# Modulation columns as dot products along the rows on VectorE, without TensorE

## The reference

```
mod = (silu(c) @ ada_w + ada_b).reshape(1, 2, 2, 3, 1024)      # ada_w is 1024 x 12288
for i in range(2):
    shift, scale, gate = mod[:, i, 0, k]
    h = rmsnorm(x, g) * (1 + scale) + shift
    y = short_conv_mixer(h) if i == 0 else ssd_mixer(h)
    x = x + gate * rmsnorm(y, g)
    shift, scale, gate = mod[:, i, 1, k]
    h = rmsnorm(x, g) * (1 + scale) + shift
    x = x + gate * rmsnorm(swiglu_ffn(h), g)
```

## Time and profile before

| | |
|---|---|
| median of three runs | 2212.21 us (2212.01 to 2213.32) |
| span of the profiled execution | 2209.9 us (the page gives no other time of that execution) |
| TensorE busy | 2167.0 us, 98% |
| VectorE, ScalarE, GpSimd busy | 1203.4, 999.4, 973.0 us |
| moved by the DMA engines | 273.88 MB, 124 GB/s on average |
| same in the first tenth | 316, 221, 209, 124 GB/s in slices of 55 us |
| mean granted clock of TensorE | 0.986 |

### The profile page before, as it was taken

How to read it: one execution, slowest core, us unless ns; L and a number is a source line. 1 busy time by engine, 2 the same in 40 slices (tenths; PEclk the granted TensorE clock), 3 DMA queues, 4 the chain that set the end, 5 groups by cost and what they waited for, 6 DMA issues and landing times.

```text
span 2209.9 us, 29015 instructions
## 1 busy us (share of the span) xinstructions
PE 2167.0 (98%) x10456; PEld 1756.4 (79%) x10456; DVE 1203.4 (54%) x1720; ACT 999.4 (45%) x1425; POOL 973.0 (44%) x421
## 2 busy tenths in 40 slices
PE   7999999999999999999999999999999899999998
PEld 5788888888878777778888888888777688888886
DVE  5877665521176877886522221240888755666522
ACT  4324544334445655654543434453555644444332
POOL 3544444446644333334544456666122143444563
PEclk8999999999999999999999999999999999999999
DMA  7653475553315344333232323344221132333232
GB/s 316 221 209 124 147 272 218 178 161 97 115 58 194 115 148 157 115 124 96 77 95 95 96 74 101 109 122 155 87 70 42 36 105 86 104 95 95 79 97 72
DMA packets 74338, 273.88 MB, mean 124 GB/s; under 512 B 8632, under 2 KB 11320, under 8 KB 67849
## 3 DMA queue, kind: packets, MB, share of 16 engines
q1 hardware_dynamic: 70872, 266.77, 36.5%
q10 hardware_dynamic: 3376, 5.90, 0.8%
HBM read 269.24 MB, written 8.12 MB: 126 GB/s over the span
## 4 chain that ended last, share of the span: by engine, by line
PE 76%; issue 14%; POOL 5%; DVE 3%; ACT 1%; DMA 1%; ACTq 0%; SPq 0%; POOLq 0%; DVEq 0%
PE bank L557 61%; POOL wlo L518 5%; PE bank L974 4%; PE bank L1066 2%; PE bank L580 2%; PE bank L1031 1%; PE bank L995 1%; PE bank L622 1%; PE bank L1014 1%; PE bank L584 1%; PE bank L630 1%; PE bank L669 1%; DMA ada_first<-ada_d 1%; DVE x L1624 1%; PE bank L915 1%
## 5 line engine op out<-in xcount | busy, mean ns | idle before, releaser
L518 POOL TENSOR_TENSOR wlo<-raw,whi 128x1024 fp32r<-128x1024 f32 x382 | 927.6, 2435 | 1146.7 <-ACT whi L1104 1146.4
L1104 ACT ACTIVATE whi<-raw 128x1024 fp32r<-128x1024 f32 x382 | 400.5, 1055 | 560.3 <-PE bank L557 537.8
L557 PE MATMUL bank<-h_hi,whi 128*128 128x512 f32 x1608 | 633.0, 394 | 1.9 <-POOL wlo L518 1.9
L557 PE MATMUL bank<-h_hi,wlo 128*128 128x512 f32 x1608 | 626.5, 390 | 0.0
L557 PE MATMUL bank<-h_lo,whi 128*128 128x512 f32 x1608 | 625.8, 389 | 0.0
L557 PEld LDWEIGHTS bank<-h_hi,whi 128*128 128x128 f32 x1608 | 301.9, 188 | 68.3 <-issue 6.3
L557 PEld LDWEIGHTS bank<-h_hi,wlo 128*128 128x128 f32 x1608 | 301.8, 188 | 64.0
L557 PEld LDWEIGHTS bank<-h_lo,whi 128*128 128x128 f32 x1608 | 302.0, 188 | 61.6
L557 PE MATMUL bank<-g_hi,whi 128*128 128x512 f32 x592 | 230.4, 389 | 0.0
L557 PE MATMUL bank<-g_hi,wlo 128*128 128x512 f32 x592 | 230.3, 389 | 0.0
L557 PE MATMUL bank<-g_lo,whi 128*128 128x512 f32 x592 | 230.3, 389 | 0.0
(11 more groups left out here) (357 smaller groups left out, 2985.2 us busy)
## 6 DMA issues: line engine op xcount, KB each, us to landing
raw<-f_in_d SPq DMA_DIRECT2D x88, 512.0 KB, 3.5
raw<-m_d SPq DMA_DIRECT2D x65, 512.0 KB, 3.6
ada_f<-ada_d SPq DMA_DIRECT2D x24, 1024.0 KB, 7.0
raw<-g_in_d SPq DMA_DIRECT2D x44, 512.0 KB, 3.5
raw<-w_in_d SPq DMA_DIRECT2D x41, 512.0 KB, 3.6
csb<-cs_d SPq DMA_DIRECT2D x32, 640.0 KB, 6.3
ada_a<-ada_d SPq DMA_DIRECT2D x16, 1024.0 KB, 4.9
raw<-a_in_d SPq DMA_DIRECT2D x24, 512.0 KB, 6.0
```

Of the source, the lines that this page charges most:

```text
L518: nc.gpsimd.tensor_tensor(wlo[:, s], raw[:, s], whi[:, s].bitcast(F32), ALU.subtract).then_inc(lo_ready, 1)
L557: mm = nc.tensor.matmul(psum[bank][:], w[:, s, kk, :], xs[part == "lo"][:, k, :], start=first and kk == 0 and i == 0, stop=last and kk == ...
L1104: nc.scalar.activation(whi[:, s], raw[:, s], ACT.Copy).then_inc(hi_ready, 1)
```

## The change

- A column of 128 outputs becomes one VectorE instruction: outputs lie in partitions, the 1024 inputs along the row. An STT over 128x1024 multiplies the weights in SBUF by silu(c), which is the same row in all partitions and lies in banks 6 and 7 of PSUM, and the row sum goes to a column of `mod` (`accum_out`). The products are written over the weights and not used.
- Weights come in another order in DRAM: a transfer of 1 MB holds two columns. The amount is the same.
- The bias is added behind a unit on VectorE, in an instruction over 128x4. `modulation`, `first_sum` and `mod_evac` are gone, and nothing of the modulation is on TensorE. Its loop in f_in0 is the one of f_in1.
- c comes by a broadcast transfer to all partitions (128 x 1024), and ScalarE writes silu(c) to PSUM at the start and again ahead of f_in0, since `residual` uses bank 6. The table's matmuls of the third block's bias move from bank 6 to bank 5.
- The first stage goes by k tile: one transfer has the shift and the scale column of tile k, eight transfers in turn with the weight chunks. For each k VectorE does two columns, bias, `ncol` and `scaled(k)`.
- The first root: ScalarE's squares are added by VectorE into `rstd`, TensorE sums them by tokens. ScalarE takes the root straight from PSUM, then splits all four weight chunks, then norms.
- VectorE's loop over f_in0 is written out.

```diff
 # SyncE, start
-            sp.dma_start(vec[:], io["vec"]).then_inc(vec_in, 16)
             for h in range(2):
                 sp.dma_start(x[:, 4 * h:4 * h + 4], ...).then_inc(x_in[h], 16)
+            sp.dma_start(cond[:].rearrange("p a n -> p (a n)"), io["c"].broadcast_to([P, D])).then_inc(c_in, 16)
+            sp.dma_start(vec[:], io["vec"]).then_inc(vec_in, 16)
+            ada_start(0)
             sp.dma_start(kst[:], io["kst"]).then_inc(kst_in, 16)
-            for v in range(2):
+            load(io["a_in"][0], 0)
+            ada_start(1)
+            for v in range(1, 4):
                 load(io["a_in"][v], v)
-            ada_start(0)
-            for v in range(2, 4):
-                load(io["a_in"][v], v)
-            for p in range(1, 4):
-                ada_start(p)
+                ada_start(v + 1)
+            for k in range(5, KD):
+                ada_start(k)
 # SyncE, later units
-                    if h or d == 4:
-                        sp.wait_ge(mod_part, d + it * n)
+                    if d == 4:
+                        sp.wait_ge(col_out, 4)
+                    elif h:
+                        sp.wait_ge(mod_part, d - 4 + it * n)
                     else:
                         sp.wait_ge(ada_half, d - 4 + it * n)
 # TensorE
             def first_root():
-                for k in range(KD):
-                    pe.wait_ge(sq_out, k + 1)
-                    nc.tensor.matmul(psum[4][:], ones[:], sq[:, k % 2, :], ...).then_inc(row_done, 1)
-                ...
+                pe.wait_ge(row_acc, KD - 1)
+                token_sums(4, rstd[:], True).then_inc(s_done, 1)
-                    if n == 0 and k % 2 == 0:
-                        first_sum(1 + k // 2)
-                    if j >= 2 and s == 0:
-                        modulation(2 + j)
             def ffn(n):
-                ...
+                four(f"f_in{n}", 1 + 2 * n)
+                with pe.Fori(0, 10) as it:
                     for u in range(4, 8):
+                        single(f"f_in{n}", u, it, 4, wait=False)
 # ScalarE
+            def condition():
+                nc.scalar.activation(silu_c, cond[:], ACT.Silu).then_inc(c_ready, 1)
+            nc.scalar.activation(root[:, SPARE, 0:1], epscol[:], ACT.Silu)
             for k in range(KD):
                 ...
+                nc.scalar.activation(sq[:, k % 2, :] if k else rstd[:], x[:, k, :], ACT.Square).then_inc(sq_out, 1)
+            act.wait_ge(c_in, 16)
+            condition()
             set_root()
-            split_hi(2)
-            act.wait_ge(s_ready, 1)
-            take_root(0, ssum[:])
-            split_hi(3)
+            act.wait_ge(s_done, 1)
+            take_root(0, psum[4][:, 0:NT])
+            for c in range(RING):
+                split_hi(c)
+            act.wait_ge(vec_in, 16)
             mod_norm(0, "a_in", 0)
             ...
             mod_norm(1, "f_in0", 1)
+            condition()
 # VectorE
+            def mod_col(t, src):
+                flat = src.rearrange("p a n -> p (a n)")
+                return STT(out=flat, in0=flat, scalar=1.0, in1=silu_c.rearrange("p a n -> p (a n)"), op0=ALU.mult, op1=ALU.mult,
+                           accum_out=mod[:, t:t + 1])
+            def mod_unit(d, ring):
+                for h in range(2):
+                    dve.wait_ge(ada_in[h], 16 * (d - 3))
+                    for e in range(2):
+                        ins = mod_col(4 * d + 2 * h + e, ring[h][:, e])
+                    ins.then_inc((ada_half, unit_out)[h], 1)
+                dve.wait_ge(unit_out, d - 3)
+                b = V0["ada_b"] + 4 * d
+                TT(mod[:, 4 * d:4 * d + 4], mod[:, 4 * d:4 * d + 4], vec[:, b:b + 4], ALU.add).then_inc(mod_part, 1)
+            def first_cols(k):
+                ins = mod_col(KD + k, ada_first[k][:, 1])
+                ins.then_inc(col_out, 1)
+                dve.wait_ge(col_out, k + 1)
+                ...
+                step(TT(pair, pair, by_kind(vec[:, b:b + 2 * KD]), ALU.add))
+                ins = STT(out=ncol[:, 0, 0, k:k + 1], in0=mod[:, KD + k:KD + k + 1], scalar=1.0, in1=V("norm_g", k), ...)
+            for k in range(1, KD):
+                dve.wait_ge(sq_out, k + 1)
+                if k >= 2:
+                    dve.wait_ge(row_acc, k - 1)
+                TT(rstd[:], rstd[:], sq[:, k % 2, :], ALU.add).then_inc(row_acc, 1)
+            dve.wait_ge(vec_in, 16)
+            dve.wait_ge(c_ready, 1)
+            for k in range(KD):
+                dve.wait_ge(first_in[k], 16)
+                ins = mod_col(k, ada_first[k][:, 0])
+                if k == 0:
+                    dve.wait_ge(std_out, 1)
+                    nc.vector.tensor_copy(ssum[:], psum[4][:, 0:NT])
                     inverse(0, R1)
+                first_cols(k)
+                if k == 0:
                     dve.wait_ge(rb_done, 1)
+                scaled(k, 4, 0, "a_in")
 # VectorE, f_in0
-                    with dve.Fori(0, 4) as it:
-                        ...
+                    dve.wait_ge(c_ready, 2)
+                    for j in range(KF):
+                        hidden(j)
+                        if j % 4 < 3 and j < 16:
+                            mod_unit(12 + 3 * (j // 4) + j % 4, ada_f)
+                        ...
```

More of the change, by code:

```diff
@@ L707, in _ @@
                     e = min(S, WB + WA - S * j)
[L708 removed]
+                    nc.tensor.matmul(psum[5][0:16, 0:e], tbl[:], hot[:, S * j:S * j + e], start=True, stop=True).then_inc(hot_sum, 1)
             for u in range(KD):
                 single("a_out", u, xs=(g_hi, g_lo))
[L711 to L712 removed]
             residual_roots(0, sums)
             def ffn(n):
[L716 to L718 removed]
+                four(f"f_in{n}", 1 + 2 * n)
+                with pe.Fori(0, 10) as it:
                     for u in range(4, 8):
[L720 to L736 removed]
+                        single(f"f_in{n}", u, it, 4, wait=False)
                 with pe.Fori(0, 2) as it:
@@ L1241, in _ @@
             ffn(0)
[L1242 removed]
+            act.wait_ge(ncol_ready, KD + 3)
             mod_norm(2, "m_in", 2)
@@ L1656, in mod_unit @@
-            def mod_unit(d, ring, it=0):
-                if d >= 5:
-                    mod_evac(d - 1, it)
-                out, half = psum[7][:], KD // 2
-                dve.wait_ge(ada_in[0], 16 * (d - 3) + it * (16 * 3))
-                step(TS(out, ring[0][:, 0, :], csil[:, 0:1], None, ALU.mult))
-                for k in range(1, half):
-                    ins = STT(out=out, in0=ring[0][:, k, :], scalar=csil[:, k:k + 1], in1=out, op0=ALU.mult, op1=ALU.add)
-                    if k < half - 1:
-                        step(ins)
-                ins.then_inc(ada_half, 1)
-                dve.wait_ge(ada_half, d - 3 + it * 3)
-                dve.wait_ge(ada_in[1], 16 * (d - 3) + it * (16 * 3))
-                for k in range(half, KD):
-                    ins = STT(out=out if k < KD - 1 else modacc[:], in0=ring[1][:, k - half, :], scalar=csil[:, k:k + 1], in1=out,
-                              op0=ALU.mult, op1=ALU.add)
-                    if k < KD - 1:
-                        step(ins)
-                ins.then_inc(mod_part, 1)
@@ L1677, in first_part @@
-            def first_part(p, h):
-                out, half = psum[6 + p % 2][:], KD // 2
-                dve.wait_ge(first_in[p][h], 16)
-                if h == 0:
-                    step(TS(out, ada_first[p][:, 0, :], csil[:, 0:1], None, ALU.mult))
-                elif p >= 2:
-                    dve.wait_ge(mod_sum, p - 1)
-                end = KD if p else DIRECT[0]
-                for k in range(max(1, half * h), min(half * (h + 1), end)):
-                    ins = STT(out=out if k < end - 1 else (modacc, acc)[p % 2][:], in0=ada_first[p][:, k, :], scalar=csil[:, k:k + 1],
-                              in1=out, op0=ALU.mult, op1=ALU.add)
-                    if k < end - 1:
-                        step(ins)
-                if h:
-                    ins.then_inc(mod_part, 1)
@@ L1789, in ffn @@
                 if n == 0:
-                    with dve.Fori(0, 4) as it:
-                        step.loop(it, 3 * (KD - 2))
-                        for j in range(4):
-                            hidden(j, it, 4)
-                            if j < 3:
-                                mod_unit(12 + j, ada_f, it)
-                        step.end(4)
-                    mod_evac(23)
-                    dve.wait_ge(mod_out, 24)
-                    gate_col(1)
-                    for q in range(2, 4):
-                        scale_col(q)
-                        gate_col(q)
-                    with dve.Fori(0, 3) as it:
-                        for j in range(16, 18):
-                            hidden(j, it, 2)
+                    dve.wait_ge(c_ready, 2)
[3 more added lines that the diff above has]
+                            mod_unit(12 + 3 * (j // 4) + j % 4, ada_f)
+                        if j == 15:
```

(5 more changed lines are left out.)

157 lines of the change are left out of this document (34 added, 123 removed).

## The result

| us | before | changed |
|---|---|---|
| median of the runs | 2212.11 (2211.16 to 2213.32) | 2186.6 (2185.34 to 2188.32) |
| profiled execution, its span | 2212.2, 2209.9 | 2188.32, 2186.5 |
| ratio, 95% interval | | 0.9884 [0.987, 0.9898] |

The kernel became 25.5 us faster; 2187 was forecast, and the forecast case is the one that came about. The profiled spans differ by 23.4 us, against 24.9 forecast.

A forecast was written before the change was run, and what follows sets the result against it. TensorE, busy 98% of the span, bounds the kernel, so only less work or fewer waits there pay. 19.2 + 5.7 = 24.9 us off the 2209.9 span gives 2185.0, plus 2.3 around it 2187 us; range 2182 to 2203.

The forecast's parts named there:

- Term 1: Removing modulation sums from TensorE in a_in, a_out and f_in0, 0.93 us each: 6.5 + 12.6 + 0.1 = 19.2 us gained.
- Sum 11: The sum behind f_in0's first four chunks, where TensorE would wait for GpSimd's low half anyway: 0.1 us, bounds 0 and 0.93.
- Term 2: VectorE's cost per modulation column: 1.22 + 0.13 = 1.35 us, upper bound 2.44, hidden behind TensorE in a_in and f_in0.
- The reserve of VectorE: In a_in, VectorE's 10 us lead and 1 us slack over 28 columns are used up at 1.75 us per column.
- rival A: Row sum doubles the column instruction to 2.4 us, so TensorE waits at a_out for g_lo[7]: 2220 us, 10%.
- Term 3: The start, with new load order and root: a_in's first four chunks end at 52.7 instead of 58.4, 5.7 us gained.
- (d): In the first stage VectorE sets the pace from k = 2, 3.65 us per k, with scaled(7) ending at 47.2.
- TensorE's slow first matmuls: In the first stage the first 15 or so matmuls take about 0.43 us each, at half the clock.
- Edits at nothing: Side edits such as silu(c) again before f_in0, bank 5 bias rows and VectorE's written-out f_in0 loop cost no time.
- B: The start gains nothing, as a_in3 lands later or the clock rises later: 2193 us, 12%.
- C: The sums were partly hidden and a wait replaces them, so half of Term 1 goes: 2197 us, 8%.

The follow-up runs named there:

- Experiment 1: Changed kernel with 20 unused groups of four one-column matmuls back on TensorE at the old places, with the old f_in0 loops: 2207.71 us, ratio 0.9972.
- experiment 4: Changed kernel with silu(c) in SBUF, written over c once, instead of PSUM, and no second computation ahead of f_in0: 2198.82 us, ratio 0.9929.
- experiment 3: Changed kernel with every modulation column multiplied by silu(c) twice on VectorE: 2205.47 us, ratio 0.9965.
- experiment 5: Changed kernel with all four a_in weight chunks loaded directly behind ada0 and ada1, ahead of ada2: 2188.75 us, ratio 0.9902.
- 6: Changed kernel with the bias of the first 16 columns copied once to PSUM bank 5 for the small addition: 2185.93 us, ratio 0.9885.
- 8: Changed kernel with experiment 5's load order, and the first columns' bias and the first norm's 8 weights in PSUM bank 5: 2182.54 us, ratio 0.9863.
- experiment 9: The changed kernel itself, unaltered, run again on another chip: 2184.22 us, ratio 0.9872 against the kernel before.

## Why the prediction was right, step by step

- **Term 1, the sums (19.2 us): right.** The seven of a_in and a_out, forecast 6.5, gave 6.7; f_in0, forecast 12.6, gave 12.6. Experiment 1 puts them back for 0.93 to 0.95 each, which in f_in0 leaves about 1.2 us for the wait that one of them had. Sum 11 was counted at 0.1, and it comes to 0.08: from the start of the last matmul of `four` to the first single chunk are 1.14 us before (255.87 to 257.01) and 1.06 now (245.36 to 246.42), since TensorE now waits 0.68 us there for GpSimd's low half.
- **Term 2, the column: right in what follows, high in size.** 1.35 was forecast; from the start of one column to the start of the next 1.14 was measured, and two columns with the gap behind them take 2.40 (36.98 to 39.38 in the timeline of VectorE). The row sum added only the read-out, which starts together with the next column. With both sources in SBUF the instruction takes 1.21 to 1.22 us undisturbed (experiment 4), the same as with one in PSUM. The Trainium skill's "Vector Engine (DVE) Microarchitecture Reference", Points that are easy to get wrong, says that two SBUF sources that aren't bf16 halve throughput, as no port is left for the accumulator; the measurement differs, and it decides. The slowdown that experiment 4 shows in SBUF is a wait for GpSimd.
- **The reserve of VectorE: wrong, and it did not matter.** It was to be used up at 1.75 us per column. At 2.40 experiment 3 finds TensorE waiting once for 2.9 us; its last g_lo starts at 188.1, where rival A had it ready only at 200.6.
- **Term 3, the start (5.7 us): 4.2 measured, the step that was mis-sized.** The landings were a little later than laid out: ada0 forecast 13.0, found 13.87; ScalarE's fourth split forecast from 25.5, found at 26.46, behind its wait for a_in3 (2.68). So the first h_hi ended at 28.22 (27.4), TensorE started at 28.27 (27.5), and scaled(2) ended 0.75 later than the 28.9 of (d). (d) then gave each k 2 x 1.35 + 0.25 + 0.7 = 3.65. 3.79 was found, with other parts: the two columns took 2.40 instead of 2.70 and scaled(k) 0.60 instead of 0.70, while the two small instructions behind the columns took 0.79 instead of 0.25, because of the addition's wait. Those 0.25 are the term that (d) had wrong in kind: it took a tiny instruction as free of GpSimd. Over the five steps that makes 0.5 us; scaled(7) ended at 48.42, 1.2 behind the 47.2, and the last 0.3 are lost behind it, where the h_lo of k = 7 was ready at 50.8 (49.5). Experiments 5, 6 and 8 show the wait at work: it grows with GpSimd's load, passes from one small instruction to the next, and is gone when neither has two SBUF operands.
- **Also in (d): TensorE's slow first matmuls.** I let 15 go at half the clock; only the first six did (28.27 to 31.0). It changed nothing. TensorE's 1.8 us of waits in the last two k tiles take it up: in experiment 9 the first twelve of the same kernel went slowly (28.15 to 33.43), and its `four` ended at 54.1 all the same.
- **Edits at nothing: right.** silu(c) ahead of f_in0 runs at 239.71, and ScalarE still waits 2.10 us for TensorE behind it:

```profile
238.41 1.28 ACT L1133 ACT_TABLE_LOAD   x1
239.71 1.03 ACT L1133 ACTIVATE bank<-cond 128x1024 f32<-128x1024 f32 x1
242.84 1.06 ACT L1049 ACTIVATE whi<-raw 128x1024 fp32r<-128x1024 f32 x1 [2.10 <-PE bank L582]
```

  VectorE holds nothing up in a_in; from 56 to 166 us it waits 9.4 us for TensorE's chunks, in place of the sums it waited for in the earlier trace rows:

```profile
L1678 DVE TENSOR_TENSOR ta<-ta,bank 128x512 f32<-128x512 f32 x7 | 4.8, 686 | 9.4 <-PE bank L555 9.4
```

- **The median, within 0.4 us of the forecast, is nearer than the working, and that is luck.** The gain of the span was forecast 1.5 too high, and executions of the changed kernel lie from 2183.65 to 2188.32 in two sets of runs.
- **Rivals.** A fell with the first row of the new instruction; had the row sum doubled it, the time would have been near 2205 (experiment 3) and not 2220, so the kernel would not have become slower at 2.2 us per column as I wrote. B (start at nothing) fell with 4.2 us, C (sums partly hidden) with f_in0 at 217.8.

## What to carry to other kernels

Price what an engine at 98% executes, not what it computes: eight tiny instructions of TensorE cost 0.95 us twenty times over, and an engine with spare time took over their work without holding anything up. When counting whether the other engine has that time, look for waits inside its busy time first: an instruction whose duration varies from 0.69 to 2.48 us is elastic, and a turn that looks full may not be. And on VectorE beside a busy GpSimd, where the second operand lies can decide more than how large it is: 128x2 in SBUF took up to 2.08 us, 128x1024 with one operand in PSUM 1.22. Check the tiny instructions on a chain as well, and move the operands of all of them, since the wait passes to the first one left.

## What the runs showed of the hardware that was not expected

- A row sum in an STT over 128x1024 costs nothing in the instruction (1.216 us against 1.222 without) and a read-out of 0.08 us; the next column starts 1.14 us after this one.
- The same STT with both operands in SBUF: 1.22 us alone, 3.40 beside GpSimd's split of a 128x1024 tile. GpSimd pays as well: in experiment 4 its h_lo takes 1.74 us in the first stage (1.29 in the changed kernel) and its split 3.25 (2.40).
- An addition over 128x2 with two SBUF operands took 0.52 to 2.08 us, and 0.16 with one in PSUM. It doesn't share with GpSimd step by step but ends within 0.03 us of the GpSimd instruction beside it (experiment 5 and the changed kernel), so its cost is what that instruction has left.
- TensorE's first matmuls after 10.6 us of waiting go in steps of 0.43 us (from 28.86 to 31.0 there are five), nearly twice the 0.227 of the full clock, while the granted clock of that stretch reads 1.00 (28.00:32.00 above). Before the change the same first steps of 0.43 stood in a stretch that read 0.50. So the two records don't tell the same there, and the step is the one to price by.
